# Masks of the sparse mixer's searched tiles: four made beside the latent mixer's last units, two inside the sparse mixer, and the search ended earlier

## The reference

```python
sc = jnp.einsum('bqhd,bsd->bqhs', qi, ki)
idx_score = jnp.einsum('bqhs,bqh->bqs', jax.nn.relu(sc), wi)
idx_score = jnp.where(chunk_mask(q_pos, k_pos)[None], idx_score, -jnp.inf)
_, sel = lax.top_k(idx_score, topk)
```

## Time and profile before

| what | value |
|---|---|
| median of 3 runs | 3221.77 us (3221.39 to 3222.02) |
| the profiled execution, its own time | 3223.93 us |
| its span, first to last instruction | 3221.7 us |
| TensorE busy in it | 2981.9 us (93%) |
| VectorE, ScalarE, GpSimd busy | 1729.8 (54%), 1278.0 (40%), 168.5 us (5%) |
| mean granted TensorE clock | 0.960 of full speed |

### The profile page before, as it was taken

The page is one execution under the profiler, slowest core; times in us unless marked ns, Lnnn a source line. Parts: engine busy times, 40 slices in busy tenths (PEclk is TensorE's granted clock), DMA queues, the critical chain, the costliest instruction groups (busy, mean ns, idle before and its releaser), DMA issues. The chain is left out here.

```text
span 3221.7 us, 48872 instructions
## 1 busy us (share of the span) xinstructions
PE 2981.9 (93%) x17421; PEld 2530.4 (79%) x17421; DVE 1729.8 (54%) x3768; ACT 1278.0 (40%) x2682; POOL 168.5 (5%) x240
## 2 busy tenths in 40 slices
PE   8976885998999999999899798988889999999998
PEld 6752553677999999999799467855679999999998
DVE  5447998754444445544431664158654444445545
ACT  4435994543222222222243454357532222222223
POOL 0000222310000000000000330000000000000000
PEclk9996997999999999999999799999999999999999
DMA  4110001021111111111311201110201111111112
GB/s 144 54 49 0 14 13 46 1 77 48 48 39 52 39 39 52 39 39 52 130 48 49 79 2 63 55 56 1 77 11 55 39 39 52 39 39 52 39 40 75
DMA packets 146190, 151.98 MB, mean 47 GB/s; under 512 B 17116, under 2 KB 122196, under 8 KB 146068
## 3 DMA queue, kind: packets, MB, share of 16 engines
q1 hardware_dynamic: 146068, 150.44, 15.2%
HBM read 126.65 MB, written 23.24 MB: 47 GB/s over the span
## 5 line engine op out<-in xcount | busy, mean ns | idle before, releaser
L223 PE MATMUL ffn_up<-hlow_r,ffn_uhi 128*128 128x384 f32 (+1 forms) x2112 | 691.1, 327 | 0.0
L2161 DVE SCALAR_TENSOR_TENSOR ffn_cv<-ffn_G,ffn_ctap,ffn_cv 128x256 f32<-128x256 f32 (+1 forms) x352 | 168.8, 500 | 493.3 <-ACT ffn_cv L2087 488.7
L223 PEld LDWEIGHTS ffn_up<-hlow_r,ffn_uhi 128*128 128x128 f32 x2112 | 398.6, 189 | 0.9
L2081 ACT ACTIVATE ffn_G<-ffn_up 128x384 f32<-128x384 f32 (+2 forms) x176 | 65.2, 397 | 825.1 <-PE ffn_up L224 825.1
L2194 DVE TENSOR_TENSOR xres<-ffn_dn,xres 128x512 f32<-128x512 f32 (+1 forms) x396 | 263.6, 687 | 132.3 <-PE ffn_dn L224 121.1
L222 PE MATMUL ffn_dn<-ffn_dhi,ffn_ahi 128*128 128x512 f32 x704 | 280.7, 399 | 2.9
L224 PE MATMUL ffn_dn<-ffn_dhi,ffn_alo 128*128 128x512 f32 x704 | 278.3, 395 | 0.0
L223 PE MATMUL ffn_dn<-ffn_dlo_r,ffn_ahi 128*128 128x512 f32 x704 | 278.3, 395 | 0.0
L222 PE MATMUL ffn_up<-mixed_c_r,ffn_uhi 128*128 128x384 f32 (+1 forms) x528 | 174.9, 331 | 5.9 <-DVE ulo_r L2138 5.9
L222 PE MATMUL ffn_up<-mixed_a_r,ffn_uhi 128*128 128x384 f32 (+1 forms) x528 | 174.6, 331 | 5.7 <-DVE ulo_r L2138 5.7
L222 PE MATMUL ffn_up<-mixed_d_r,ffn_uhi 128*128 128x384 f32 (+1 forms) x528 | 174.3, 330 | 0.0
(11 more groups left out here) (473 smaller groups left out, 6944.2 us busy)
## 6 DMA issues: line engine op xcount, KB each, us to landing
ulo<-in_w_up_dram SPq DMA_DIRECT2D x44, 512.0 KB, 5.0
ffn_ulo<-in_w_up_dram SPq DMA_DIRECT2D x44, 512.0 KB, 4.6
ffn_dlo<-in_w_down_dram SPq DMA_DIRECT2D x22, 1024.0 KB, 4.9
w_d<-in_w_in_odd_dram SPq DMA_DIRECT2D x7, 768.0 KB, 10.3
proj_even_x<-in_x_prompt_dram SPq DMA_DIRECT2D x8, 512.0 KB, 3.4
xres<-in_x_prompt_dram SPq DMA_DIRECT2D x8, 512.0 KB, 4.5
scratch_x<-xres SPq DMA_DIRECT2D x8, 512.0 KB, 3.5
x_d<-scratch_x SPq DMA_DIRECT2D x8, 512.0 KB, 3.9
```

Of the source, the lines that this page charges most:

```text
L223: nc.tensor.matmul(out, lh, rl, start=False, stop=False)
L2081: s.activation(G[:, g0:g0 + w], upbank(c, b, 0)[:, j:j + w], ACT.Copy).then_inc(g_out, 1)
L2161: last = v.scalar_tensor_tensor(cv[:, 0, j:j + w], G[:, g0 - 2 + tapno:g0 - 2 + tapno + w], ctap[:, c, tapno:tapno + 1], cv[:, 0, j:j + w] ...
```

## The change

The search gets one step in each unit from 0 to 29 and a second one in units 16 and 25 (t = 7 of the second and third pair), and so ends in unit 29 where it ended in unit 32. `next_float` is in unit 30 and `room_for_ties` in unit 31. Units 32 to 35 make the masks of tiles 2, 3, 4 and 5, a whole mask each, ahead of the last output. The masks of tiles 6 and 7 are made in mixer A, one of the five operations in each of its first ten units, and the scratch for them lies there. Mixer A runs two units ahead instead of three (as "c" did), and takes tiles 0 to 5 of the first two pairs, then tiles 6 and 7 of these pairs, then the rest as before. Its rounds for the sample move to units 12 to 21, the sample's mask to unit 22.

```diff
-SAMPLE_LAST = [(p, t) for p in range(PAIRS) for t in range(NT)] + [(p, NT) for p in range(PAIRS)]
+SAMPLE_LAST = ([(p, t) for p in range(2) for t in range(6)] + [(p, t) for p in range(2) for t in (6, 7)] +
+               [(p, t) for p in range(2, PAIRS) for t in range(NT)] + [(p, NT) for p in range(PAIRS)])
...
-TWICE, ONCE = (6, 7), (1, 2, 3, 4, 5)
+TWICE, SEARCH_ENDS = (16, 25), 29
...
-    for i, (p, t) in enumerate(ALL):
-        n = min(STEPS - done, 2 if t in TWICE else 1 if t in ONCE else 0)
+    for i in range(len(ALL)):
+        n = (2 if i in TWICE else 1) if i <= SEARCH_ENDS else 0
...
+CHOSEN_B = {32: 2, 33: 3, 34: 4, 35: 5}
+CHOSEN_A = (6, 7)
+ROUNDS_FROM = 12
...
-        ahead = 2 if fox else 3
+        if mla or dsa:
+            top, work, spare, told = src["top"], src["work"], src["top"]["spare"], sem("told")
+            scratch = below if mla else sb("scratch", [P, 2 * SEQ], BF16)
+            tie, beyond = scratch[:, 0:SEQ], scratch[:, SEQ:2 * SEQ]
+        ahead = 3 if stick or mla else 2
...
+                if dsa and t in CHOSEN_A:
+                    dve.wait_ge(told, FROM + 5 * CHOSEN_A.index(t) + 5)
...
-                if dsa and 0 < i <= rounds:
-                    best_scores(i - 1)
+                if dsa and ROUNDS_FROM <= i < ROUNDS_FROM + rounds:
+                    best_scores(i - ROUNDS_FROM)
...
                 if mla and i == SEARCH_ENDS + 1:
                     next_float()
+                if mla and i == SEARCH_ENDS + 2:
                     room_for_ties()
-                if mla and i > SEARCH_ENDS + 1:
-                    select(i - SEARCH_ENDS - 2)
+                if mla and i in CHOSEN_B:
+                    for part in range(5):
+                        select(CHOSEN_B[i], 8 + 5 * (i - SEARCH_ENDS - 3), part)
+                if dsa and i < 5 * len(CHOSEN_A):
+                    select(CHOSEN_A[i // 5], 5 * (i // 5), i % 5)
             output(n_units - 1)
-            if mla:
-                for j in range(n_units - SEARCH_ENDS - 2, n_top):
-                    select(j)
```

More of the change, by code:

```diff
@@ L873 @@
 STEPS = 32
-TWICE, ONCE = (6, 7), (1, 2, 3, 4, 5)
+TWICE, SEARCH_ENDS = (16, 25), 29
 def search_steps():
     at, done = {}, 0
-    for i, (p, t) in enumerate(ALL):
-        n = min(STEPS - done, 2 if t in TWICE else 1 if t in ONCE else 0)
+    for i in range(len(ALL)):
+        n = (2 if i in TWICE else 1) if i <= SEARCH_ENDS else 0
         at[i] = list(range(done, done + n))
         done += n
+    assert done == STEPS
     return at
 SEARCH_AT = search_steps()
-SEARCH_ENDS = max(i for i in SEARCH_AT if SEARCH_AT[i])
+CHOSEN_B = {32: 2, 33: 3, 34: 4, 35: 5}
+CHOSEN_A = (6, 7)
+ROUNDS_FROM = 12
 class Groups:
@@ L952, in attention @@
             v = [sb(f"v{s}", [P, KT, P]) for s in range(2)]
-            top, work, n_top = src["top"], src["work"], len(SEARCHED)
+            n_top = len(SEARCHED)
             wide = [0] + [sum(key_tile(t)[0] for t in SEARCHED[:j + 1]) for j in range(n_top)]
             below = sb("below", [P, wide[-1]], BF16)
-            tie, beyond = below[:, 0:SEQ], below[:, SEQ:2 * SEQ]
-            spare, up = sb("spare", [P, n_top]), sb("up", [P, n_top], mybir.dt.int32)
+            up = sb("up", [P, n_top], mybir.dt.int32)
             counted = {"dve": sem("counted_dve"), "act": sem("counted_act")}
-            settled, cand_ready, told = sem("settled"), sem("cand_ready"), sem("told")
-        ahead = 2 if fox else 3
+            settled, cand_ready = sem("settled"), sem("cand_ready")
+        if mla or dsa:
[3 more added lines that the diff above has]
+        ahead = 3 if stick or mla else 2
         ring = ahead + 1
@@ L1396, in room_for_ties, with select @@
                 dve.wait_ge(told, FROM + 8)
-            def select(j):
-                t = SEARCHED[j]
-                w, n = work[t][:], key_tile(t)[0]
+            def select(t, told_before, part):
+                j, n = SEARCHED.index(t), key_tile(t)[0]
+                w = work[t][:]
                 out = src["bias"][:, src["bias_at"][t]:src["bias_at"][t] + n]
@@ L1404, in select @@
                 tied, left_over = tie[:, 0:n], beyond[:, 0:n]
[L1405 to L1414, removed]
+                if part == 0:
+                    dve.wait_ge(told, FROM + told_before)
+                    v_.tensor_scalar(tied, w, bar, -TIE, ALU.is_equal, ALU.mult).then_inc(told, 1)
+                elif part == 1:
+                    v_.tensor_scalar(out, w, bar, -TIE, ALU.is_lt, ALU.mult).then_inc(told, 1)
+                elif part == 2:
+                    dve.wait_ge(told, FROM + told_before + 1)
+                    v_.tensor_tensor_scan(left_over, tied, tied, spare[:, j:j + 1], ALU.add, ALU.bypass).then_inc(told, 1)
+                elif part == 3:
+                    dve.wait_ge(told, FROM + told_before + 3)
+                    v_.scalar_tensor_tensor(left_over, left_over, 0.0, tied, ALU.is_lt, ALU.mult).then_inc(told, 1)
+                else:
+                    dve.wait_ge(told, FROM + told_before + 4)
+                    v_.tensor_tensor(out, left_over, out, ALU.add).then_inc(told, 1)
             if stick:
@@ L1459, in _ @@
                     output(i - 1)
-                if dsa and 0 < i <= rounds:
-                    without_best(i - 1)
-                if dsa and i == rounds + 1:
+                if dsa and ROUNDS_FROM <= i < ROUNDS_FROM + rounds:
+                    without_best(i - ROUNDS_FROM)
+                if dsa and i == ROUNDS_FROM + rounds:
                     sample_mask()
@@ L1493, in search_state @@
     return {"cnt": sb("top_cnt", [P, n]), "limit": sb("top_limit", [P, n]), "over": sb("top_over", [P, n]),
-            "bits": sb("top_bits", [P, n], I32), "cand": sb("top_cand", [P, n], I32), "ok": sb("top_ok", [P, n], I32)}
+            "bits": sb("top_bits", [P, n], I32), "cand": sb("top_cand", [P, n], I32), "ok": sb("top_ok", [P, n], I32),
+            "spare": sb("top_spare", [P, n])}
 def load_up(eng, dram, soon, p):
```

## The result

The changed kernel takes 3205.91 us (median of 5 runs, 3200.57 to 3206.48), the kernel before 3222.02 beside it (3221.39 to 3225.62): ratio 0.9944, 95% interval 0.9931 to 0.9958. The forecast was 3207.0. The profiled execution took 3206.48 us for a span of 3204.3, 17.4 less than the span before.

The account below looks back on a forecast made before the run. VectorE alone, making masks, was taken to bound the seam between the latent and sparse mixers. Terms -21.1 + 3 + 0.5 + 2.8 = -14.8 gave 3207.0 us on the median's scale, range 3199 to 3217.

Parts of the forecast that it names:

- Last pair, 21.1 less: Latent mixer's last pair and tail: 41.3 us against 62.4, by masks moved out, steps moved forward and less idleness.
- Pairs before, 3 more: Latent mixer's earlier pairs: t=5 and first t=6 rows fall, t=8 and t=0 rise; 3 us more, bounds -4 and +7.
- First unit, 0.5 more: Latent mixer's first unit: its added search step is covered but for 0.5 us, bounds 0 to 1.5.
- Sparse mixer, 2.8 more: Sparse mixer's sum: scans 2.5 more, ring 2 more, prologue 1.7 less, order 0.
- Their excess is 1.1 + 1.4: 2.5 more: Sparse mixer: the two mask scans exceed VectorE's free 0.95 us per unit, costing 2.5 us; bounds 0 and 11.
- the ring of three: Sparse mixer two units ahead with three probability buffers: 0.5 us a pair, 2 more in all; bounds 0 and 7.6.
- The prologue: Sparse mixer's start with two units: first reciprocal comes at 537.30 instead of 539.03, 1.7 us less.
- The order at 0: Sparse mixer's new order of units leaves every product in place: 0.
- A: Rival: latent mixer has no room, only the 11.0 us of masks moved out count; 3214 to 3221, chance 0.13.
- B: Rival: sparse mixer's masks and GpSimd's scaling exclude each other at ten meetings, 5.9 us more, 3213; chance 0.12.
- C: Rival: slower, the ring of three shows in the sparse mixer; at 0.8 us a unit 3234; chance 0.05.
- D: Rival: all evens out, the latent mixer's pairs gain 3 us and the ring is free; 3199 to 3201, chance 0.12.

Follow-up runs that it names:

- experiment 3: Kernel before with the changed latent mixer only, masks of t=6 and 7 behind its last output, sparse mixer as before: 3214.82 us, ratio 0.9965 to 0.9986.
- experiment 4: Changed kernel with the masks of tiles 6 and 7 left out of the sparse mixer: 3201.92 us, ratio 0.9921 to 0.9951.
- 5: Changed kernel with each of the sparse mixer's two scans replaced by two counts with one SBUF input: 3206.61 us, ratio 0.9938 to 0.9969.
- experiment 7: Changed kernel with the sparse mixer's ten mask operations in other units, scans in the fifth and tenth: 3203.30 us, ratio 0.9932 to 0.9959.
- experiment 1: Kernel before with only the sparse mixer two units ahead and a ring of three probability buffers: 3217.52 us, ratio 0.9979 to 0.9998.
- experiment 2: Kernel before with only the sparse mixer's new order of tiles: 3219.49 us, ratio 0.9985 to 1.0006.
- 6: Changed kernel with the second reciprocals of units 33, 34 and 35 ahead of the search's closing and masks: 3204.40 us, ratio 0.9933 to 0.9960.

## Why the prediction was right, point by point

**The forecast's mechanism holds**: VectorE's masks at the seam were the bound, and filling the mixers with them removes it. The stretch fell by 15.8 in the profile, where the sum said 14.8. That the two are so near is in part luck: in the profile the last pair gave 1.2 less than forecast and the pairs before cost 0.7 more, while the sparse mixer came out 3.0 better.

**Last pair, 21.1 less.** In the profile 42.5 us from 478.06 to the last mask's end, where I had 41.3. The first half is exact (24.25 for 24.3). The second took 18.2 instead of 17.0: the 0.8 for a waiting copy became 1.90, and one mask operation took 1.30 us at 504.26, beside GpSimd's scalings (501.60 to 505.16), where wider operations of its kind take 0.69 (512) and 0.82 (640). I had looked for that contention in the sparse mixer only. The 1.90 goes with the clock, 0.50 in that unit: in the kernels of experiments 3 to 5, at 0.64 to 0.66, the copy waits 0.87 to 1.02 us and the last pair, to its last output copy, takes 41.1 to 41.6 instead of 42.4. So the term holds to within what the clock moves.

**Pairs before, 3 more.** Measured 3.7 (160.5 us for three, 156.8 before); over the six kernels with this schedule 1.4 to 3.8, on average 2.5. The size is right, **its first term is not**: "the t=5 row falls from 7.88 to TensorE's 5.05" gave 7.18, 5.78 and 7.27. I let TensorE take over as soon as VectorE was relieved; but the row had ScalarE busy for 7.17 too. ScalarE's timeline in the third pair:

```profile
446.51 1.15 ACT L1251 ACTIVATE att_b_below<-scores,top_cand 128x1024 bf16<-128x1024 f32 x1
...
448.45 0.62 ACT L1251 ACTIVATE att_b_below<-scores,top_cand 128x384 bf16<-128x384 f32 x1
...
449.05 1.08 ACT L1185 ACTIVATE att_b_pt<-att_b_tp 128x512 f32<-128x512 f32 x2
```

and TensorE's:

```profile
449.70 0.68 PE L1131 MATMUL att_b_tp<-ident,att_b_prob 128*128 128x128 f32 x3 [1.04 <-ACT att_b_pt L1185]
450.18 2.08 PE L1115 MATMUL att_b_tp<-wkv,latT 128*128 128x128 f32 x8
```

Its three counts stand ahead of the copies of the transposes, TensorE waits 1.04 us, and afterwards runs at the lower clock (eight products from `wkv` took 2.08 us, 1.16 in the pair where it stayed up). Over the six kernels 15 of the 18 rows of t=5 took 5.76 to 5.78 us at full clock with ScalarE busy from end to end, the other three 7.2 to 7.3 at 0.76 and 0.77. So ScalarE keeps back 0.7 of the 2.8, and the lower clock another 1.4 where it comes. What made up for it: t=8 rose to 4.86, not 5.5, t=0 to 5.8 on average, not 6.2, and the first pair's t=6 fell to 5.33 (6.0 in the other five kernels), not 6.67.

**First unit, 0.5 more**: 0.3 in this profile, 0.6 on average.

**Sparse mixer, 2.8 more.** Measured 0.2 less: two steps erred against each other, the masks costing more than forecast, the ring and the prologue less. "Their excess is 1.1 + 1.4: 2.5 more" was too small: 3.9 (experiment 4), of which 0.8 are the operations behind the scans, which I had put at nothing. The free time of 0.95 a unit came from a mean of two units; the units that got the scans had 0.5 to 0.6, and where there is 1.6 the scan costs 0.3 (experiment 7). "I take 0.5 a pair, 2 more" for the ring of three **failed by its sign**: depth two takes about 1 off the body of the mixer (experiment 1: 4.2 in all, 3.2 of it in the prologue). I had priced depth as cover that is lost and carried a figure over from another mixer, without asking what the 1.90 of idleness a pair in the earlier trace rows waited for; the waits would have said: peaks. The prologue gave 2.9 instead of 1.7 (9.74 us against 12.59), although its clock was the lowest, 0.50. The order at 0 holds (experiment 2). By the runs the masks' 3.9 and the depth's -4.2 make -0.3, where the change measured -0.2.

**The seam** came as written: 5.33 us of pause with 4.4 of masks in it, scans in the third and eighth unit with TensorE idle beside each (0.62 and 1.52 us first), later pairs of the sparse mixer at 30.25.

**Rivals.** A falls by experiment 3, B by 5 and 7, C by 1. Of D the free ring was true, and more than free; the gain in the pairs wasn't.

## What to carry to other kernels

Work that an engine does alone at a seam is worth its whole length there, and only its excess over the engine's free time in the unit that takes it: give the longest operation to the unit with the most slack, read unit by unit, not as a mean. When one engine is relieved in a row, look at the second busiest and at what stands ahead in its queue before handing the bound to TensorE. Of a pipeline's depth read what the idleness waits for now, before costing a smaller one.

## What was not expected of the hardware

A stage that no edit touched has two durations, and the granted clock in one stretch of it tells them apart. The stick-breaking mixer's stage table, 70 to 80 us after its start, before:

```profile
2195.33:2205.33 10.00, 6.81 (x57) 5.08 (x56) 8.21 (x14) 4.08 (x12) 0.00 (x0) 0.83 0.01 2
```

and after:

```profile
2181.09:2191.09 10.00, 6.81 (x79) 5.45 (x79) 8.16 (x14) 5.48 (x16) 0.00 (x0) 1.00 0.01 2
```

In these 10 us TensorE's busy time is the same, the granted clock is 0.83 in the one and 1.00 in the other, and 57 products fit where 79 did. Whole, the stage takes 166.99 and 163.86 us; over the whole of it the clock averages 0.94 in both. All nine kernels show one of the two pairs of figures: 0.83 and 167 us before and in experiments 1, 4 and 7, 1.00 and 163.9 us after and in 2, 3, 5 and 6. That goes with none of the edits, and what decides it no run shows. So where two totals differ by 3 us, look at the stretch that was changed.
